# One 512-column matmul for both input parts of a feature-major weight block, the halves summed at the eviction

## The chip, the cores and the metric

One core of one Trainium2 chip runs the whole program in one launch. The metric is the device time of that launch in microseconds. TensorE (PE in the profile) multiplies, VectorE (DVE), ScalarE (ACT) and GpSimd (POOL) work on elements, and SyncE (SP) issues all DMAs.

## The reference

A block with a gated delta rule, an S5 state space part, cross attention and a SwiGLU feed-forward, then a second block with two layers (stick-breaking and block attention, then forgetting attention), each with a cross attention of four small heads and a feed-forward with a convolution. 256 positions, model width 1024, all in float32. The linear layers and feed-forwards are what the change touches:

```python
def _swiglu(hn, w_gate, w_up, w_down):
    return (jax.nn.silu(hn @ w_gate) * (hn @ w_up)) @ w_down

def conv_ffn(h, w_up, conv_w, conv_b, w_down):
    u = h @ w_up
    up = jnp.pad(u, ((0, 0), (CONV_WIDTH_2 - 1, 0), (0, 0)))
    c = conv_b
    for i in range(CONV_WIDTH_2):
        c = c + up[:, i:i + S] * conv_w[i]
    gate, val = c[..., :D_FF_2], c[..., D_FF_2:]
    return (jax.nn.silu(gate) * val) @ w_down
```

Every `hn` is a root mean square norm of the residual stream; the hidden width is 2816 = 22 tiles of 128. The other matrices are 1024 x 1024 (`w_out`, `w_xk`, `w_xq`, `w_xo`, q, k and output of the two mixers) or 1024 x 256 and 256 x 1024 (the small cross attentions), and `w_in`, `glu` and the values.

## The kernel before, in words

All activations lie feature-major in SBUF: 128 features of a tile on the partitions, T = 256 positions as columns, 8 such tiles for the model width. The weights come as 342 slots of 8 blocks of 128 x 128; SyncE loads one slot after the other in the order of use.

From `x_v` on the products keep nearly float32 accuracy by splitting. ScalarE rounds a slot to float32r (`w_hi`, L1127), VectorE subtracts that from the raw weights (`w_lo`, L1686). Every third slot's low part is made by GpSimd instead (L2500, `lo_on_pool`); in the feed-forwards that is the gate's slot. `SPLIT_SLOTS` = 3 split slots exist, so each engine's helper `ahead(s)` makes slots up to s + 2 at written places of its own order, and ScalarE waits until TensorE has read the slot three back. The inputs are split in the same way into `a_hi`, `a_lo` (tiles `AH`, `AL`) or `b_hi`, `b_lo` (`BH`, `BL`). A product of one block is three matmuls, made by `three` (L418): high weights with high input, high weights with low input, low weights with high input, all added in the same 256 columns of a PSUM bank.

A feature-major layer (`fm`, and gate and up in `ffn`) sums K input tiles (8, or 2 in `m_o0` and `m_o1`) for each of its output tiles in one bank, taken in turn from two (`acc_take` waits until the bank's last eviction). The evictions are VectorE's. In `scaled` (L1858, for q and k) and in `ffn` (L2245) one operation multiplies the bank with the norm factor `R` into SBUF; in `residual` (L2115) one adds the bank to `H`. After a residual tile ScalarE makes the next layer's `a_hi` (L1153) and the square (L1143), VectorE `a_lo` (L1698) and the sum of squares (L2105).

`ffn` goes through f = 0 to 22. TensorE's order: gate f, up f (8 blocks each), down f - 1 (8 blocks from `B`, still `three`, into banks 4 to 7). VectorE's order for f in the stages with convolution (ffn1, ffn2): evict gate; wait for ScalarE's first convolution term (L1569); two convolution steps (L2250, L2252); the same for up; product of gate and up (L2264); low part of a weight slot; low part of the activation (L2273); low part of another weight slot. ScalarE's order: first term for gate, weight copy of the next gate (which GpSimd waits for), first term for up, silu (L1574), weight copy, high part of the activation (L1584), weight copy. ffn0 has no convolution steps. Each engine runs its queue strictly in this written order; semaphores tie them. The helper `step` puts a wait on VectorE's own semaphore behind an operation, so that the next reads its result.

The functions that the diff touches:

## Time and profile before

| | us |
|---|---|
| median of 3 runs | 1260.03 |
| lowest, highest | 1256.9, 1260.96 |
| the profiled execution | 1257.22 |
| its span in the trace | 1255.3 |
| TensorE busy | 1194.8 |
| VectorE busy | 808.1 |
| ScalarE busy | 656.8 |
| GpSimd busy | 265.0 |

The stages, in us from the start of the span: w_in and the memory's small projections to 141, x_v and x_k among the delta rule to 247, w_out to 273, x_q and attention to 313, x_o to 340, ffn0 to 527, the first mixer (ab) to 640, ab_o to 665, the small cross attention to 695, ffn1 to 885, the forgetting mixer (fox) to 998, fox_o to 1020, the small cross attention to 1050, ffn2 to 1241. Busy times of matmuls overlap in the pipeline: what counts for TensorE is the distance between the starts of two matmuls.

### The profile page before, as it was taken

How to read it: one execution, taken by the hardware profiler on the slowest of the kernel's cores; microseconds unless marked ns; L12 is line 12 of the kernel's file. 1: busy time of each engine (PE TensorE's matmuls, PEld its weight loads, DVE VectorE, ACT ScalarE, POOL GpSimd, SP SyncE). 2: the span in 40 equal slices, each digit the busy share in tenths (PEclk: the TensorE clock that was granted, in tenths of full speed). 3: DMA queues.
4: the chain of work that ended last, by engine and by line, in shares of the span. 5: the costliest groups of instructions: out<-in, count | busy, mean ns of one | idle time of the engine just before them, and what ended most of it. 6: DMA issues, size and time to landing. Idle time of an engine off the chain costs nothing.

```text
span 1255.3 us, 24604 instructions
## 1 busy us (share of the span) xinstructions
PE 1194.8 (95%) x10064; PEld 1119.2 (89%) x10064; DVE 808.1 (64%) x1426; ACT 656.8 (52%) x1128; POOL 265.0 (21%) x172
## 2 busy tenths in 40 slices
PE   7999999899999999999998899999999988999997
PEld 6888778799899999998886899999889877999997
DVE  4886655564655454567866677677665576776776
ACT  3443633653644444465455655555655566555554
POOL 4030000121222322321120222322221211232231
PEclk9999899999999999999999999999999999999999
DMA  8443322353565565643343466565443342656651
GB/s 320 128 134 119 108 96 86 101 169 101 155 199 175 181 189 181 184 135 102 117 135 102 119 200 176 181 192 178 150 141 116 115 151 84 187 182 187 181 176 48
DMA packets 51518, 187.58 MB, mean 149 GB/s; under 512 B 5712, under 2 KB 5840, under 8 KB 51024
## 3 DMA queue, kind: packets, MB, share of 16 engines
q1 hardware_dynamic: 51408, 186.02, 47.8%
q8 instruction: 80, 1.31, 0.4%
q14 instruction: 30, 0.25, 0.1%
HBM read 184.95 MB, written 1.05 MB: 148 GB/s over the span
## 4 chain that ended last, share of the span: by engine, by line
PE 83%; DVE 7%; ACT 4%; issue 3%; POOL 1%; DMA 0%; DVEq 0%; SPq 0%; ACTq 0%
PE banks L418 62%; PE banks L448 7%; ACT w_hi L1127 2%; PE banks L491 2%; DVE w_lo L1686 1%; PE banks L476 1%; PE banks L924 1%; PE banks L938 1%; POOL w_lo L2500 1%; DVE h L2115 1%; PE banks L539 1%; PE banks L904 1%; DVE gates L2105 1%; PE banks L841 1%; DVE a_lo L1698 1%
## 5 line engine op out<-in xcount | busy, mean ns | idle before, releaser
L418 PE MATMUL banks<-a_hi,w_hi 128*128 128x256 f32 x1432 | 412.2, 288 | 10.1 <-ACT arena L1426 4.2
L2500 POOL TENSOR_TENSOR w_lo<-w_raw,w_hi 128x1024 fp32r<-128x1024 f32 x99 | 240.6, 2430 | 836.0 <-ACT w_hi L1127 836.0
L1127 ACT ACTIVATE w_hi<-w_raw 128x1024 fp32r<-128x1024 f32 x313 | 328.4, 1050 | 157.4 <-PE banks L418 157.3
L418 PE MATMUL banks<-a_lo,w_hi 128*128 128x256 f32 x1432 | 405.9, 283 | 0.0
L418 PE MATMUL banks<-a_hi,w_lo 128*128 128x256 f32 x1432 | 405.8, 283 | 0.0
L1686 DVE TENSOR_TENSOR w_lo<-w_raw,w_hi 128x1024 fp32r<-128x1024 f32 x214 | 264.5, 1236 | 66.7 <-ACT w_hi L1127 66.5
L418 PEld LDWEIGHTS banks<-a_hi,w_hi 128*128 128x128 f32 x1432 | 275.4, 192 | 14.9 <-ACT arena L1426 4.6
L418 PEld LDWEIGHTS banks<-a_lo,w_hi 128*128 128x128 f32 x1432 | 275.5, 192 | 0.4
L418 PEld LDWEIGHTS banks<-a_hi,w_lo 128*128 128x128 f32 x1432 | 275.3, 192 | 0.0
L418 PE MATMUL banks<-b_hi,w_hi 128*128 128x256 f32 x880 | 254.9, 290 | 16.2 <-DVE h L2115 3.9
L418 PE MATMUL banks<-b_hi,w_lo 128*128 128x256 f32 x880 | 249.9, 284 | 0.0
L418 PE MATMUL banks<-b_lo,w_hi 128*128 128x256 f32 x880 | 249.9, 284 | 0.0
L418 PEld LDWEIGHTS banks<-b_hi,w_hi 128*128 128x128 f32 x880 | 169.5, 193 | 22.4 <-issue 12.2
L418 PEld LDWEIGHTS banks<-b_lo,w_hi 128*128 128x128 f32 x880 | 169.7, 193 | 0.3
L418 PEld LDWEIGHTS banks<-b_hi,w_lo 128*128 128x128 f32 x880 | 169.6, 193 | 0.0
L1569 ACT ACTIVATE arena<-arena,pars 128x256 f32<-128x256 f32 x88 | 53.0, 602 | 132.9 <-DVE arena L2245 132.9
L2245 DVE TENSOR_TENSOR arena<-banks,rstd 128x256 f32<-128x256 f32 x132 | 55.8, 423 | 103.2 <-PE banks L418 93.4
L448 PE MATMUL banks<-early,w_raw 128*128 128x256 f32 x400 | 92.2, 390 | 7.6 <-DMA w_raw<-in_weights 7.6
L2250 DVE SCALAR_TENSOR_TENSOR arena<-arena,pars 128x255 f32<-128x255 f32 x88 | 59.1, 672 | 60.7 <-ACT arena L1569 60.7
L448 PEld LDWEIGHTS banks<-early,w_raw 128*128 128x128 f32 x400 | 77.0, 195 | 19.4 <-DMA w_raw<-in_weights 7.6
L1153 ACT ACTIVATE a_hi<-h,pars 128x256 fp32r<-128x256 f32 x64 | 32.5, 507 | 63.4 <-DVE h L2115 53.3
L1584 ACT ACTIVATE b_hi<-arena 128x256 fp32r<-128x256 f32 x66 | 27.6, 418 | 36.6 <-DVE arena L2264 36.6
(379 smaller groups left out, 1326.7 us busy)
## 6 DMA issues: line engine op xcount, KB each, us to landing
w_raw<-in_weights SPq DMA_DIRECT2D x342, 512.0 KB, 3.6
h<-in_x SPq DMA_DIRECT2D x1, 1024.0 KB, 5.1
arena<-in_mem SPq DMA_DIRECT2D x1, 1024.0 KB, 12.3
early<-in_mem SPq DMA_DIRECT2D x1, 1024.0 KB, 14.3
out_h<-h SPq DMA_DIRECT2D x4, 256.0 KB, 2.7
cons<-in_cons SPq DMA_DIRECT2D x1, 546.0 KB, 7.6
arena<-in_late SPq DMA_DIRECT2D x1, 448.0 KB, 4.2
pars<-in_pars SPq DMA_DIRECT2D x1, 290.5 KB, 2.7
```

Source lines behind the costliest of these rows:

```text
L418: ins = mm(out, l, r, start=start and n == 0, stop=stop and n == 2, skip_group_check=check)
L448: ins = mm(out, raw(s, b % 8), x[:, k, :], start=n == 0, stop=n == K - 1)
L476: ins = mm(out, x[:, k, cols], raw(s, b * w % 8, w), start=k == 0, stop=k == K - 1)
L491: ins = mm(bank[2][:, 0:T] if out is None else out, ONES_D[:] if by is None else by, squares, start=m == 0, stop=m == KD - 1)
L1127: do(WHI[:, n % SPLIT_SLOTS, :], RAW[:, n % RAW_SLOTS, :], ACT.Copy).then_inc(*inc("w_hi_made", ("w_hi", n)))
L1153: do(x[0][:, m, :], src, ACT.Copy, scale=par(g, m)).then_inc(*inc("input_hi", ("a_hi", tag, m)))
L1569: do(FC[:, 2 * (f % 2) + g, :], FS[:, 2 * (f % 3) + g, :], ACT.Identity, scale=par(f"cw{conv}", 88 + g * NF + f), bias=par(f"cb{conv}", g ...
L1584: do(BH[:, f % 3, :], FA[:, f % 2, :], ACT.Copy).then_inc(*inc("ffn_act_hi", ("act_hi", tag, f)))
L1686: v.tensor_tensor(WLO[:, n % SPLIT_SLOTS, :], RAW[:, n % RAW_SLOTS, :], WHI[:, n % SPLIT_SLOTS, :].bitcast(F32), ALU.subtract).then_inc(*i ...
L2245: v.tensor_tensor(x, acc(t)[:, 0:T], R[:], ALU.mult).then_inc(*inc("ffn_scaled", ("fs", tag, f, g), ("acc", t)))
L2250: step(v.scalar_tensor_tensor(c[:, 1:T], x[:, 0:T - 1], par(f"cw{conv}", 44 + g * NF + f), c[:, 1:T], ALU.mult, ALU.add), label="ffn_conv")
L2500: g.tensor_tensor(WLO[:, n % SPLIT_SLOTS, :], RAW[:, n % RAW_SLOTS, :], WHI[:, n % SPLIT_SLOTS, :].bitcast(F32), ALU.subtract).then_inc(*i ...
```

## The change

`AH`, `AL` become the two halves of one tile `A`, `BH`, `BL` those of `B`. A new `joint` multiplies a block's high weights with both input parts in one matmul of 2 x 256 columns, which fills a whole bank: high times high in the first half, high times low in the second. The low weights with the high input are added to the first half by a second matmul of 256 columns. All feature-major split layers use it but `glu` and `fox_f` (`ONE_HALF`); the token-major layers and the down products keep `three`. At the eviction the two halves are added: in `scaled` and `ffn` by a `tensor_reduce` over the halves from PSUM to SBUF, a wait, and then the multiplication in SBUF; in `residual` by two additions one after the other. The layers before `x_v`, with whole weights, are as before.

```diff
@@ -235,8 +235,8 @@
                 "p (a b) -> p a b", a=KD) for i in range(3))
         WHI = sb("w_hi", [P, SPLIT_SLOTS, 1024], F32R)
         WLO = sb("w_lo", [P, SPLIT_SLOTS, 1024], F32R)
-        AH, AL = sb("a_hi", [P, KD, T], F32R), sb("a_lo", [P, KD, T], F32R)
-        BH, BL = sb("b_hi", [P, KD, T], F32R), sb("b_lo", [P, KD, T], F32R)
+        A, B = (sb(n, [P, 2, KD, T], F32R) for n in ("a_parts", "b_parts"))
+        (AH, AL), (BH, BL) = ((x[:, 0, :, :], x[:, 1, :, :]) for x in (A, B))
         RAW = sb("w_raw", [P, RAW_SLOTS, 1024])
         H = sb("h", [P, KD, T])
         K1, V1 = sb("k1", [P, KD, T]), sb("v1", [P, TT, D])
@@ -292,8 +292,9 @@
 
             return bank[(6, 6, 6, 6, 6, 2, 3, 4)[p]]
 
-        A = (AH, AL)
-        B = (BH, BL)
+        def halves(key):
+
+            return acc(key).rearrange("p (a b) -> p a b", a=2)
 
 
         QKV = area(0, 12, T)
@@ -418,12 +419,19 @@
                     ins = mm(out, l, r, start=start and n == 0, stop=stop and n == 2, skip_group_check=check)
                 return ins
 
+            def joint(out, w, x, k, start, stop):
+
+
+                mm(out.rearrange("p (a b) -> p a b", a=2), w[0], x[:, :, k, :], start=start, stop=stop,
+                   skip_group_check=True)
+                return mm(out[:, 0:T], w[1], x[:, 0, k, :], start=False, stop=stop, skip_group_check=True)
+
             def blocks(s, b, n=1):
                 c = slice(b * P, (b + n) * P)
                 return WHI[:, s % SPLIT_SLOTS, c], WLO[:, s % SPLIT_SLOTS, c]
 
             def pair(x, k, cols=slice(0, T)):
-                return x[0][:, k, cols], x[1][:, k, cols]
+                return x[:, 0, k, cols], x[:, 1, k, cols]
 
             def raw(s, b, n=1):
                 return RAW[:, s % RAW_SLOTS, b * P:(b + n) * P]
@@ -432,7 +440,7 @@
 
 
                 K = SHAPE[name][0]
-                out = acc_take((name, m))[:, 0:T]
+                out = acc_take((name, m))
                 for n, k in enumerate(range(K)):
                     b = m * K + k
                     s = SLOT[name, b // 8]
@@ -445,9 +453,11 @@
                             sums(k)
                         pe.wait_ge(*at(x_ready(k)))
                     if whole(s):
-                        ins = mm(out, raw(s, b % 8), x[:, k, :], start=n == 0, stop=n == K - 1)
+                        ins = mm(out[:, 0:T], raw(s, b % 8), x[:, k, :], start=n == 0, stop=n == K - 1)
+                    elif name in ONE_HALF:
+                        ins = three(out[:, 0:T], blocks(s, b % 8), pair(x, k), n == 0, n == K - 1)
                     else:
-                        ins = three(out, blocks(s, b % 8), pair(x, k), n == 0, n == K - 1)
+                        ins = joint(out, blocks(s, b % 8), x, k, n == 0, n == K - 1)
                     ev = ([("slot", s)] if (m * K + n) % 8 == 7 else []) + ([(name, m)] if n == K - 1 else [])
                     if ev:
                         ins.then_inc(*inc("product_done", *ev))
@@ -862,12 +872,12 @@
                 for f in range(NF + 1):
                     if f < NF:
                         for g in range(2):
-                            out = acc_take((name, 2 * f + g))[:, 0:T]
+                            out = acc_take((name, 2 * f + g))
                             slot_ready(s)
                             for k in range(KD):
                                 if f == 0 and g == 0:
                                     pe.wait_ge(*at(("a_lo", tag, k)))
-                                ins = three(out, blocks(s, k), pair(A, k), k == 0, k == KD - 1)
+                                ins = joint(out, blocks(s, k), A, k, k == 0, k == KD - 1)
                             ins.then_inc(*inc("product_done", ("slot", s), (name, f, g)))
                             s += 1
                             if f == 0 and g == 0:
@@ -1146,11 +1156,11 @@
                 act.wait_ge(*at(ready))
                 if after:
                     act.wait_ge(*at(after))
-                do(x[0][:, m, :], src, ACT.Copy).then_inc(*inc("input_hi", (key, tag, m)))
+                do(x[:, 0, m, :], src, ACT.Copy).then_inc(*inc("input_hi", (key, tag, m)))
 
             def hi_gained(tag, m, x, src, g, ready):
                 act.wait_ge(*at(ready))
-                do(x[0][:, m, :], src, ACT.Copy, scale=par(g, m)).then_inc(*inc("input_hi", ("a_hi", tag, m)))
+                do(x[:, 0, m, :], src, ACT.Copy, scale=par(g, m)).then_inc(*inc("input_hi", ("a_hi", tag, m)))
 
             def rstd(tag, dst, src=None, scale=1.0, rows=slice(0, P)):
 
@@ -1695,12 +1705,12 @@
 
             def lo_gained(tag, m, x, src, g):
                 dve.wait_ge(*at(("a_hi", tag, m)))
-                v.scalar_tensor_tensor(x[1][:, m, :], src, par(g, m), x[0][:, m, :].bitcast(F32),
+                v.scalar_tensor_tensor(x[:, 1, m, :], src, par(g, m), x[:, 0, m, :].bitcast(F32),
                                        ALU.mult, ALU.subtract).then_inc(*inc("input_lo", ("a_lo", tag, m)))
 
             def lo(tag, m, x, src, key=("a_hi", "a_lo")):
                 dve.wait_ge(*at((key[0], tag, m)))
-                v.tensor_tensor(x[1][:, m, :], src, x[0][:, m, :].bitcast(F32), ALU.subtract).then_inc(
+                v.tensor_tensor(x[:, 1, m, :], src, x[:, 0, m, :].bitcast(F32), ALU.subtract).then_inc(
                     *inc("input_lo", (key[1], tag, m)))
 
             v.memset(ONES_D[:], 1.0 / D).then_inc(*inc("vector_step", "ones"))
@@ -1855,8 +1865,14 @@
             def scaled(name, m, dst, r, scale=1.0):
                 t = (name, m)
                 dve.wait_ge(*at((name, m)))
-                v.scalar_tensor_tensor(dst, acc(t)[:, 0:T], scale, r, ALU.mult, ALU.mult).then_inc(
-                    *inc("scaled_out", (name, "scaled", m), ("acc", t)))
+                if whole(SLOT[name, 0]):
+                    v.scalar_tensor_tensor(dst, acc(t)[:, 0:T], scale, r, ALU.mult, ALU.mult).then_inc(
+                        *inc("scaled_out", (name, "scaled", m), ("acc", t)))
+                    return
+                step(v.tensor_reduce(dst, halves(t).rearrange("p a b -> p b a"), AX.X, ALU.add), ("acc", t),
+                     label="halves_summed")
+                v.scalar_tensor_tensor(dst, dst, scale, r, ALU.mult, ALU.mult).then_inc(
+                    *inc("scaled_out", (name, "scaled", m)))
 
 
             turn = delta_banks(bank)
@@ -2112,7 +2128,8 @@
                     ahead(FIRST[name] + (m * K + K - 1) // 8)
                     t = (name, m)
                     dve.wait_ge(*at((name, m)))
-                    step(v.tensor_tensor(H[:, m, :], H[:, m, :], acc(t)[:, 0:T], ALU.add),
+                    step(v.tensor_tensor(H[:, m, :], H[:, m, :], halves(t)[:, 0, :], ALU.add), label="halves_summed")
+                    step(v.tensor_tensor(H[:, m, :], H[:, m, :], halves(t)[:, 1, :], ALU.add),
                          ("h", tag, m), ("acc", t), label="h_made")
                     if m:
                         lo_gained(tag, m - 1, A, H[:, m - 1, :], g)
@@ -2242,8 +2259,9 @@
                                 dve.wait_ge(*at(("fa", tag, f - 3)))
                             x = FS[:, 2 * (f % 3) + g, :]
                             t = (name, 2 * f + g)
-                            v.tensor_tensor(x, acc(t)[:, 0:T], R[:], ALU.mult).then_inc(
-                                *inc("ffn_scaled", ("fs", tag, f, g), ("acc", t)))
+                            step(v.tensor_reduce(x, halves(t).rearrange("p a b -> p b a"), AX.X, ALU.add), ("acc", t),
+                                 label="halves_summed")
+                            v.tensor_tensor(x, x, R[:], ALU.mult).then_inc(*inc("ffn_scaled", ("fs", tag, f, g)))
                             if conv is not None:
                                 c = FC[:, 2 * (f % 2) + g, :]
                                 dve.wait_ge(*at(("fc", tag, f, g)))
@@ -2579,6 +2597,8 @@
 
 SUMMED = ("xa", "f0", "xa0", "xa1")
 
+ONE_HALF = ("glu", "fox_f")
+
 POOL_SUMMED = ("mem1", "mem2")
 
 sq_before = {}
```

## Rows read from the trace of the kernel before

**Rows 1.** Page, parts 1 and 4: busy time; chain that ended last.
```profile
PE 1194.8 (95%) x10064; PEld 1119.2 (89%) x10064; DVE 808.1 (64%) x1426; ACT 656.8 (52%) x1128; POOL 265.0 (21%) x172
...
PE 83%; DVE 7%; ACT 4%; issue 3%; POOL 1%; DMA 0%; DVEq 0%; SPq 0%; ACTq 0%
```

**Rows 2.** Windows: stretch, its us, each engine's busy us, PE clock, DMA share.
```profile
340.00:527.00 187.00, 186.65 (x1546) 185.91 (x1547) 93.76 (x142) 88.01 (x119) 52.89 (x22) 1.00 0.61 185
527.00:640.00 113.00, 109.94 (x781) 96.65 (x781) 82.84 (x125) 62.91 (x110) 21.79 (x9) 1.00 0.42 124
...
695.00:885.00 190.00, 186.87 (x1551) 186.21 (x1549) 134.56 (x218) 106.50 (x156) 52.82 (x22) 1.00 0.59 175
...
1050.00:1241.00 191.00, 188.68 (x1555) 187.93 (x1553) 134.12 (x217) 106.25 (x156) 52.85 (x22) 0.99 0.53 160
```

**Rows 3.** Timeline of PE in ffn1: start, duration, operation; 256-column matmuls.
```profile
699.82 0.28 PE L418 MATMUL banks<-a_hi,w_hi 128*128 128x256 f32 x1
...
701.98 0.28 PE L418 MATMUL banks<-a_hi,w_hi 128*128 128x256 f32 x1
```

**Rows 4.** Timeline of PE in the token-major x_v: 512-column matmuls.
```profile
158.57 0.39 PE L418 MATMUL banks<-w_hi,b_lo 128*128 128x512 f32 x1
...
160.86 0.40 PE L418 MATMUL banks<-w_lo,b_hi 128*128 128x512 f32 x1
```

**Rows 5.** Timeline of VectorE, one period of ffn1.
```profile
784.17 0.42 DVE L2245 TENSOR_TENSOR arena<-banks,rstd 128x256 f32<-128x256 f32 x1 [0.16 <-PE banks L418]
785.26 0.49 DVE L2250 SCALAR_TENSOR_TENSOR arena<-arena,pars 128x255 f32<-128x255 f32 x1 [0.67 <-ACT arena L1569]
785.79 0.48 DVE L2252 SCALAR_TENSOR_TENSOR arena<-arena,pars 128x254 f32<-128x254 f32 x1
787.05 0.42 DVE L2245 TENSOR_TENSOR arena<-banks,rstd 128x256 f32<-128x256 f32 x1 [0.78 <-PE banks L418]
788.15 0.80 DVE L2250 SCALAR_TENSOR_TENSOR arena<-arena,pars 128x255 f32<-128x255 f32 x1 [0.67 <-ACT arena L1569]
...
792.81 0.42 DVE L2245 TENSOR_TENSOR arena<-banks,rstd 128x256 f32<-128x256 f32 x1 [0.17 <-PE banks L418]
```

**Rows 6.** Timeline of ScalarE in the same period.
```profile
784.63 0.60 ACT L1569 ACTIVATE arena<-arena,pars 128x256 f32<-128x256 f32 x1 [1.88 <-DVE arena L2245]
785.14 1.05 ACT L1127 ACTIVATE w_hi<-w_raw 128x1024 fp32r<-128x1024 f32 x1
```

**Rows 7.** Timeline of GpSimd in the same period.
```profile
786.26 2.40 POOL L2500 TENSOR_TENSOR w_lo<-w_raw,w_hi 128x1024 fp32r<-128x1024 f32 x1 [6.24 <-ACT w_hi L1127]
```

**Rows 8.** VectorE groups by line and shape: count, busy us, mean ns, idle.
```profile
L2264 DVE TENSOR_TENSOR arena<-arena 128x256 f32<-128x256 f32 x66 | 30.6, 464 | 6.1 <-ACT arena L1574 0.2
...
L2115 DVE TENSOR_TENSOR h<-h,banks 128x256 f32<-128x256 f32 x48 | 19.9, 415 | 7.9 <-PE banks L418 7.5
L1858 DVE SCALAR_TENSOR_TENSOR arena<-banks,rstd 128x256 f32<-128x256 f32 x44 | 18.6, 422 | 37.7 <-PE banks L418 31.9 <-ACT rstd L1160 5.6
...
L2171 DVE TENSOR_REDUCE small<-banks 128x2 f32<-128x512 f32 x12 | 8.2, 680 | 0.0
```

**Rows 9.** Line views of L2250 and L2245: minimum, median and maximum ns.
```profile
L2250 DVE SCALAR_TENSOR_TENSOR arena<-arena,pars x88: 482/486/1644, 700.0 to 1238.9; 128x255 f32<-128x255 f32 x88
...
L2245 DVE TENSOR_TENSOR arena<-banks,rstd x132: 411/424/425, 343.6 to 1237.8; 128x256 f32<-128x256 f32 x132
```

**Rows 10.** Timeline of VectorE in w_out's output and residual.
```profile
259.48 0.41 DVE L2115 TENSOR_TENSOR h<-h,banks 128x256 f32<-128x256 f32 x1
...
262.86 0.41 DVE L2115 TENSOR_TENSOR h<-h,banks 128x256 f32<-128x256 f32 x1
...
266.76 2.16 DVE L1686 TENSOR_TENSOR w_lo<-w_raw,w_hi 128x1024 fp32r<-128x1024 f32 x1 [1.18 <-ACT w_hi L1127]
268.84 0.41 DVE L2115 TENSOR_TENSOR h<-h,banks 128x256 f32<-128x256 f32 x1
```

**Rows 11.** Timeline of GpSimd in the same stretch.
```profile
265.15 2.69 POOL L2500 TENSOR_TENSOR w_lo<-w_raw,w_hi 128x1024 fp32r<-128x1024 f32 x1 [7.01 <-ACT w_hi L1127]
```

## The prediction

> **What bounds the kernel now.** I read the page first: TensorE is busy for 1194.8 of 1255.3 us and carries 83% of the chain that ended last, VectorE 7% [rows 1]. So a shorter matmul stream is worth something, if nothing else is close behind. That is a question for each stage, so next comes the windows view by stage [rows 2]: in all three feed-forward stages TensorE is busy to within 3 us of the stretch. Beside it VectorE works 93.8 of 187 us in ffn0, but 134.6 of 190 in ffn1 and 134.1 of 191 in ffn2. The third view is the timeline of one period (one hidden tile f) of ffn1 [rows 5]: the first eviction repeats after 792.81 - 784.17 = 8.64 us, exactly 72 matmuls of 0.120 us, so TensorE sets the period. What the reader should see is how little VectorE has left: its only waits for TensorE are 0.78 us before the second eviction and 0.17 us before the next first one, 0.95 us together. Its other waits (0.67 us twice) are for ScalarE's first convolution step, which itself waits for the eviction. They don't shrink when more work is put on VectorE.
>
> **What the change takes from TensorE.** Each feature-major weight block had three matmuls of 256 columns; now it has one of 512 and one of 256. A 256-column matmul starts every (701.98 - 699.82) / 18 = 0.120 us [rows 3]. A 512-column one, in the token-major layer, starts every (160.86 - 158.57) / 10 = 0.229 us [rows 4]. At 2.4 GHz (granted clock 1.00 [rows 2]) the columns alone are 0.107 and 0.213 us, so each instruction costs about 0.013 us beyond its columns, and one fewer saves 0.240 - 0.229 = 0.011 to 0.013 us. I take 0.012. Blocks: gate and up 3 x 22 x 16 = 1056; w_out, x_k, x_q, x_o, ab_o, fox_o 64 each = 384; ab_q, ab_k, fox_q, fox_k 64 each = 256; m_q0, m_o0, m_q1, m_o1 16 each = 64; in all 1760. 1760 x 0.012 = 21.1 us is all that TensorE can give back. The down products (528 blocks), glu and fox_f keep three matmuls. The new 512 columns are read from two places 2048 elements apart, which no row here shows; bounds for it are no saving at all (as if it were two matmuls) and the full one. I take the full one, because only the start of a second run changes.
>
> The Trainium skill (TensorE: Matmul & The Clock Gate, What's actually happening) gives a fixed cost of about 2.5 ns for each back-to-back matmul. By it the saving would be 1760 x 0.0025 = 4.4 us in place of 21.1. The rows show 13 ns, and I stay with them; either way it is a small term here.
>
> **What it puts on VectorE.** (a) An eviction of `ffn` or `scaled` was one operation from PSUM, 0.42 us (L1858 and L2245) [rows 8, 9]. It becomes a sum of 512 PSUM elements, then a wait on its own semaphore, then a product from SBUF. Nearest rows: a reduce of 512 PSUM elements takes 0.68 us (L2171), a 256-element product from two SBUF operands 0.43 us at its minimum (L2264, mean 0.464) [rows 8], and a step that waits for the one before starts 0.04 us after it (785.75 to 785.79) [rows 5]. So 0.68 + 0.04 + 0.43 = 1.15, or +0.73 us. The sum reads the two halves alternately; if that costs up to as much again, it is 1.2 us. From below: (0.68 - 0.42) / 256 = 1.0 ns per element between the two sizes, so 512 elements without anything fixed are 0.52. I take 0.68, since L2171 has the same count and source. The bank is free 0.26 us later than before, and the product that takes it starts over 5 us later: nothing. Behind the new wait stands the product on VectorE, and ScalarE's convolution step (L1569) waits for that; in `scaled`, the scores' matmuls. (b) A residual gets a second add, 0.415 + 0.04 = +0.45 us (L2115) [rows 8].
>
> **Where (a) lies on the path: the feed-forward with convolution.** Count from the first eviction of a period [rows 5, 6]. Before, the second convolution step ends 786.27 - 784.17 = 2.10 us after the eviction starts; after, 2.10 + 0.73 = 2.83. TensorE finishes up's product 2.8 us after gate's, so VectorE goes on without its 0.78 us wait, and the second sum runs from 2.83 to 3.51. GpSimd's share of the weight split is released by ScalarE's copy, which follows the first ScalarE convolution step (785.14 + 1.05 = 786.19); it begins at 786.26, just as the second convolution step ends [rows 5 to 7]. That order is kept, because both hang on the same ScalarE step: GpSimd reads SBUF from 2.83 to 5.23 (2.40 us). Now the new product: it has two SBUF inputs. What such an operation does beside GpSimd stands in the fifth row of [rows 5]: L2250, issued at 788.15 while GpSimd ran until 788.66 [rows 7], ended at 788.95 and took 0.80 instead of 0.49 us; its maximum is 1.64 [rows 9]. In the timeline it was long in every one of the 42 cases that met GpSimd. The old eviction, with one SBUF input, met GpSimd too (787.05) and never took more than 0.425 us in 132 [rows 9]. So the product, ready at 3.55, is held until GpSimd ends and finishes at 5.23 + 0.29 = 5.52. Then as before: 0.68 to the convolution step, 0.49 for it (it no longer meets GpSimd) = 6.69, and from its end (788.95) to where VectorE was free for the next eviction (792.64) 3.69, in all 10.38 us. TensorE needs 16 x 0.348 + 8 x 0.360 = 8.45. So VectorE sets the period: +1.7 us each, 21 periods after the first, two stages: 42 x 1.7 = +71 us. TensorE waits at the next gate's and up's low weights.
>
> The Trainium skill (SBUF — State Buffer, Who interferes with whom) states the rule behind it: a VectorE instruction with two SBUF inputs contends with a GpSimd instruction that reads SBUF, and the one that starts second is blocked entirely. It speaks against this change, and the trace agrees (0.80 and 1.64 against 0.49 us). Without that rule the sum would be the second rival below.
>
> **The other stages.** ffn0 has no convolution: VectorE's 93.8 us [rows 2] + 44 x 0.73 = 126 of 183 us, and even with a hold of 2 us in each of 22 periods 170. TensorE stays the bound: 22 x 16 x 0.012 = -4.2 us. Residuals: in w_out, three tiles take 268.84 - 259.48 = 9.36 us [rows 10] against 8.64 of TensorE, so a chain already sets the pace: residual, ScalarE's copy and square, its weight copy, the low part (on VectorE, or on GpSimd at 265.15 with the following VectorE one held to 268.92), next residual [rows 10, 11]. The add is in it twice for three tiles, and a third time where it pushes the gained low part into GpSimd's time: +0.9 to 1.3 per three tiles, +3 us for eight, four such stages: +12. m_o0 and m_o1 have products of 0.7 us a tile and VectorE nearly without pause: 8 x 0.45 less the waits, +2.5 each: +5. Where scores wait for a scaled tile at a stage's end (x_q, ab, fox, m_q0, m_q1), +0.7 each: +3. x_k and x_q save 0.8 each, given back in part: -1. In ab VectorE is busy 82.8 of 113 [rows 2]; 16 x 0.73 = 12 more, against 1.5 saved; I take +4 (between -1.5 and +12); fox has more room, 0.
> Sum: -4.2 + 71 + 12 + 5 + 3 - 1 + 4 = +90 us. The profiled execution took 1257.2 us (span 1255.3 and 1.9 around it), the median of the runs is 1260.0, so I add the sum to the first and half the difference: 1348 us.
>
> **Rivals.** (1) The sum over alternating halves is slow (1.2 us). In the convolution stages only the first of a pair lengthens the period, since the second hides beneath the hold: 42 x 0.52 = 22, and 5 elsewhere: 1375 us. Nothing in the rows speaks for it or excludes it. (2) The product isn't held. Period 2.83 + 1.15 + 0.68 + 0.49 + 3.69 = 8.84, +0.2 x 42 = 8 in place of 71: 1285 us. Against it: the 42 of 42. (3) Faster: VectorE's additions are hidden and TensorE alone counts, 1257.2 - 21.1 = 1236 us. It decides at a VectorE period under 8.45 us; even without the hold it is 8.84, so this needs operations about 0.2 us shorter each than their rows, and no GpSimd conflict. (4) The 512-column matmul runs as two: the 21.1 us aren't there, but only ffn0 and little else shows it: +6, 1354 us, inside the forecast's own range of 1320 to 1375.
>
> **How the numbers follow.** Forecast with (4) 0.72; (1) 0.12; (2) 0.11; (3) 0.05. The range 1290 to 1385 takes in the forecast, nearly all of (1) and the upper edge of (2). Under 0.3% (3.8 us), which is about what a measurement of this kernel can tell from no change, either way: 0.02, the edge between (2) and (3). Faster 0.05, slower 0.93.
>
> **What would show it.** In ffn1's timeline: starts 0.23 and 0.12 us apart on TensorE and 1 to 2 us of waiting for low weights in each period; a period near 10.4 us; the second product of a pair near 2 us long and ending 0.3 us after GpSimd, the first 0.43; ffn0 at 8.45 us a period; three residual tiles in some 10.5 us. A second product of 0.43 us makes (2) true, a reduce over 1 us (1), an unchanged period of matmul starts (4).

## The result

| | before | changed kernel |
|---|---|---|
| median | 1259.82 us (4 runs, 1256.9 to 1260.96) | 1351.56 us (4 runs, 1348.37 to 1354.01) |
| ratio of the times | | 1.0736, 95% interval 1.0709 to 1.0762 |
| span of the profiled execution | 1255.3 us | 1351.5 us |

The changed kernel is slower by 7.4%, some 92 us; the forecast was 1348 us, in a range of 1290 to 1385.

First the page of the changed kernel (parts 1 and 4: busy time by engine, and the chain that ended last), which answers to [rows 1], and the windows view of most of ffn1, to [rows 2]:

```profile
PE 1214.0 (90%) x8304; PEld 1031.7 (76%) x8304; DVE 1005.6 (74%) x1658; ACT 660.1 (49%) x1128; POOL 264.4 (20%) x172
...
PE 45%; DVE 40%; ACT 10%; issue 4%; DMA 0%; DVEq 0%; SPq 0%; ACTq 0%
```

```profile
711.00:929.00 218.00, 189.80 (x1177) 165.69 (x1176) 182.89 (x257) 102.37 (x150) 48.03 (x21) 0.99 0.46 151
```

1760 matmuls fewer, VectorE 197.5 us busier (time in which one of its operations is held counts as busy), and the chain that ended last is now VectorE's for 40% where it was 7%. In ffn1 VectorE works 182.9 of 218 us, and TensorE is no longer busy to the edge of the stretch.

One period of ffn1, VectorE's timeline (start, duration, operation), which answers to [rows 5]. L2262 is the sum of the halves, L2264 the product with the norm factor:

```profile
803.03 0.68 DVE L2262 TENSOR_REDUCE arena<-banks 128x256 f32<-128x512 f32 x1
803.75 0.42 DVE L2264 TENSOR_TENSOR arena<-arena,rstd 128x256 f32<-128x256 f32 x1
804.85 0.48 DVE L2268 SCALAR_TENSOR_TENSOR arena<-arena,pars 128x255 f32<-128x255 f32 x1 [0.67 <-ACT arena L1579]
805.37 0.48 DVE L2270 SCALAR_TENSOR_TENSOR arena<-arena,pars 128x254 f32<-128x254 f32 x1
805.77 0.68 DVE L2262 TENSOR_REDUCE arena<-banks 128x256 f32<-128x512 f32 x1
806.49 2.02 DVE L2264 TENSOR_TENSOR arena<-arena,rstd 128x256 f32<-128x256 f32 x1
809.17 0.48 DVE L2268 SCALAR_TENSOR_TENSOR arena<-arena,pars 128x255 f32<-128x255 f32 x1 [0.67 <-ACT arena L1579]
...
813.26 0.68 DVE L2262 TENSOR_REDUCE arena<-banks 128x256 f32<-128x512 f32 x1
```

GpSimd's timeline of the same period (to [rows 7]):

```profile
805.84 2.38 POOL L2518 TENSOR_TENSOR w_lo<-w_raw,w_hi 128x1024 fp32r<-128x1024 f32 x1 [7.85 <-ACT w_hi L1137]
```

TensorE's timeline, those of its rows in the period that waited:

```profile
808.37 0.47 PE L425 MATMUL banks<-a_parts,w_hi 128*128 128x512 f32 x1 [0.69 <-POOL w_lo L2518]
...
811.97 0.47 PE L425 MATMUL banks<-a_parts,w_hi 128*128 128x512 f32 x1 [0.59 <-DVE w_lo L1696]
```

The period is 813.26 - 803.03 = 10.23 us, against 8.64. No row of VectorE in it waits for TensorE any more. The second product, issued at 806.49, ends at 808.51, 0.29 us after GpSimd's operation (805.84 + 2.38 = 808.22); the first, which meets nothing, takes 0.42. TensorE is the one that waits, at the next gate's low weights from GpSimd and the next up's from VectorE.

The line views of the two operations (minimum, median, maximum ns), to [rows 9]:

```profile
L2262 DVE TENSOR_REDUCE arena<-banks x132: 676/684/693, 349.0 to 1330.8; 128x256 f32<-128x512 f32 x132
```

```profile
L2264 DVE TENSOR_TENSOR arena<-arena,rstd x132: 424/425/2520, 349.7 to 1331.6; 128x256 f32<-128x256 f32 x132
```

TensorE's timeline in ffn0, where it is the bound (to [rows 3, 4]):

```profile
449.74 0.40 PE L425 MATMUL banks<-a_parts,w_hi 128*128 128x512 f32 x1
449.98 0.28 PE L427 MATMUL banks<-a_parts,w_lo 128*128 128x256 f32 x1
450.10 0.40 PE L425 MATMUL banks<-a_parts,w_hi 128*128 128x512 f32 x1
...
450.44 0.40 PE L425 MATMUL banks<-a_parts,w_hi 128*128 128x512 f32 x1
...
450.80 0.40 PE L419 MATMUL banks<-b_parts,w_hi 128*128 128x256 f32 x2
```

A block takes (450.80 - 449.74) / 3 = 0.353 us, not the 0.348 foreseen.

And VectorE's timeline in w_out (to [rows 10]), L2131 being the first of the two adds:

```profile
260.93 0.41 DVE L2131 TENSOR_TENSOR h<-h,banks 128x256 f32<-128x256 f32 x1
261.38 0.42 DVE L2132 TENSOR_TENSOR h<-h,banks 128x256 f32<-128x256 f32 x1
```

```profile
267.72 2.59 DVE L2121 TENSOR_TENSOR gates<-gates,squares 128x256 f32<-128x256 f32 x1
...
271.37 0.41 DVE L2131 TENSOR_TENSOR h<-h,banks 128x256 f32<-128x256 f32 x1
```

Three tiles take 271.37 - 260.93 = 10.44 us there, against 9.36. L2121 is the sum of squares; beside GpSimd it takes 2.59 us.

The span by stretches, from the start of the first to the start of the last eviction of a stage (in ffn the last up's), in us. "Between" is everything else: the front, the attention parts, the small cross attentions and the ends of the feed-forwards; the lines below it are its largest differences:

| stretch | before | changed | difference | foreseen |
|---|---|---|---|---|
| ffn0 | 180.3 | 178.8 | -1.5 | -4.2 |
| ffn1 and ffn2 | 184.0, 184.2 | 217.4, 217.4 | +66.6 | +71 |
| w_out, x_o, ab_o, fox_o | 22.3, 22.5, 22.6, 20.6 | 24.5, 24.6, 24.5, 22.4 | +8.0 | +12 |
| m_o0, m_o1 | 8.9, 8.9 | 11.7, 11.3 | +5.1 | +5 |
| between | 601.1 | 619.1 | +18.0 | +6 |
| of it ahead of ab_o | 117.8 | 120.2 | +2.4 | |
| of it ahead of m_o0 | 19.8 | 21.7 | +1.9 | |
| of it ahead of fox_o | 116.3 | 121.6 | +5.3 | |
| of it ahead of m_o1 | 20.5 | 23.7 | +3.2 | |
| of it after ffn2's last eviction | 17.5 | 20.7 | +3.1 | |

### The profile page after: what moved, and what is told of

It reads as the page before. It is cut to its first block, busy times and chain, and to the rows that moved or that the text cites. A ratio compares the mean times of both kernels' runs of the same rounds, so it can differ in the third digit from the quotient of the medians.

```text
span 1351.5 us, 21316 instructions
## 1 busy us (share of the span) xinstructions
PE 1214.0 (90%) x8304; PEld 1031.7 (76%) x8304; DVE 1005.6 (74%) x1658; ACT 660.1 (49%) x1128; POOL 264.4 (20%) x172
## 4 chain that ended last, share of the span: by engine, by line
PE 45%; DVE 40%; ACT 10%; issue 4%; DMA 0%; DVEq 0%; SPq 0%; ACTq 0%
PE banks L425 11%; DVE w_lo L1696 11%; PE banks L419 11%; DVE arena L2264 8%; PE banks L456 7%; PE banks L427 5%; DVE arena L2262 4%; ACT arena L1579 4%; DVE arena L2268 3%; DVE arena L2270 3%; ACT w_hi L1137 2%; PE banks L501 1%; DVE arena L2282 1%; DVE h L2132 1%; DVE gates L2121 1%
## 5 line engine op out<-in xcount | busy, mean ns | idle before, releaser
L425 PE MATMUL banks<-a_parts,w_hi 128*128 128x512 f32 x1408 | 517.0, 407 | 59.7 <-POOL w_lo L2518 29.8
L427 PE MATMUL banks<-a_parts,w_lo 128*128 128x256 f32 x1408 | 396.2, 281 | 0.0
L425 PEld LDWEIGHTS banks<-a_parts,w_hi 128*128 128x128 f32 x1408 | 266.3, 189 | 141.1 <-issue 70.3
L427 PEld LDWEIGHTS banks<-a_parts,w_lo 128*128 128x128 f32 x1408 | 268.0, 190 | 0.5
L419 PE MATMUL banks<-b_parts,w_hi 128*128 128x256 f32 x1056 | 195.9, 286 | 14.4 <-DVE b_parts L2291 9.2
L419 PEld LDWEIGHTS banks<-b_parts,w_hi 128*128 128x128 f32 x1056 | 165.8, 193 | 18.5 <-issue 10.0
L419 PE MATMUL banks<-b_parts,w_lo 128*128 128x256 f32 x528 | 150.6, 285 | 0.0
L425 PE MATMUL banks<-b_parts,w_hi 128*128 128x512 f32 x352 | 132.8, 416 | 18.8 <-POOL w_lo L2518 9.1
L2264 DVE TENSOR_TENSOR arena<-arena,rstd 128x256 f32<-128x256 f32 x132 | 128.3, 972 | 4.6
L2262 DVE TENSOR_REDUCE arena<-banks 128x256 f32<-128x512 f32 x132 | 90.5, 686 | 47.4 <-PE banks L427 37.3
L419 PEld LDWEIGHTS banks<-b_parts,w_lo 128*128 128x128 f32 x528 | 101.8, 193 | 0.0
L427 PE MATMUL banks<-b_parts,w_lo 128*128 128x256 f32 x352 | 99.6, 283 | 0.0
L425 PEld LDWEIGHTS banks<-b_parts,w_hi 128*128 128x128 f32 x352 | 67.1, 191 | 41.3 <-issue 12.9
L427 PEld LDWEIGHTS banks<-b_parts,w_lo 128*128 128x128 f32 x352 | 67.6, 192 | 0.3
```

Source lines behind the costliest of these rows:

```text
L419: ins = mm(out, l, r, start=start and n == 0, stop=stop and n == 2, skip_group_check=check)
L425: mm(out.rearrange("p (a b) -> p a b", a=2), w[0], x[:, :, k, :], start=start, stop=stop, skip_group_check=True)
L427: return mm(out[:, 0:T], w[1], x[:, 0, k, :], start=False, stop=stop, skip_group_check=True)
L2262: step(v.tensor_reduce(x, halves(t).rearrange("p a b -> p b a"), AX.X, ALU.add), ("acc", t), label="halves_summed")
L2264: v.tensor_tensor(x, x, R[:], ALU.mult).then_inc(*inc("ffn_scaled", ("fs", tag, f, g)))
```

## The experiments

The theory: in ffn1 and ffn2 VectorE became the bound, and most of it is one operation of a period, the second product, that is held while GpSimd reads SBUF. The rivals: it is the amount of work on VectorE alone; or the 512-element sum; or TensorE. The kernel before was measured again beside each set of runs, with medians of 1255.9 to 1259.8 us, so the ratios to it say more than differences of a few us between two versions.

**The product with one SBUF input.** The same two operations of the same size, only the sum goes to a half bank of PSUM that is free in the feed-forwards:

```diff
-                            step(v.tensor_reduce(x, halves(t).rearrange("p a b -> p b a"), AX.X, ALU.add), ("acc", t),
+                            s_ = bank[3][:, g * T:(g + 1) * T]
+                            step(v.tensor_reduce(s_, halves(t).rearrange("p a b -> p b a"), AX.X, ALU.add), ("acc", t),
                                  label="halves_summed")
-                            v.tensor_tensor(x, x, R[:], ALU.mult).then_inc(*inc("ffn_scaled", ("fs", tag, f, g)))
+                            v.tensor_tensor(x, s_, R[:], ALU.mult).then_inc(*inc("ffn_scaled", ("fs", tag, f, g)))
```

> The changed kernel, but gate's and up's sum of the two halves is written to a free half bank of PSUM instead of SBUF, so that the product with the norm factor has one SBUF input; count and size of the operations are the same. Theory 1 (the product with two SBUF inputs is held by GpSimd's reading operation): every product takes 0.42 us; the hold moves on to the second convolution step of up, which still meets GpSimd's last 0.6 us, so the period of ffn1 and ffn2 falls from 10.23 to 9.1 us and the total from 1352 by 42 x 1.14 to about 1303 us. Theory 2 (it is the amount of VectorE work and the semaphore wait alone): the period stays 10.2 and the total 1352 us.

Measured: 1306.10 us, ratio to the kernel before 1.0392 (1.0375 to 1.0410) against 1.0736. Its VectorE timeline in ffn1, and GpSimd's:

```profile
784.99 0.69 DVE L2263 TENSOR_REDUCE banks<-banks 128x256 f32<-128x512 f32 x1
...
787.73 0.69 DVE L2263 TENSOR_REDUCE banks<-banks 128x256 f32<-128x512 f32 x1
788.46 0.42 DVE L2265 TENSOR_TENSOR arena<-banks,rstd 128x256 f32<-128x256 f32 x1
789.55 0.93 DVE L2269 SCALAR_TENSOR_TENSOR arena<-arena,pars 128x255 f32<-128x255 f32 x1 [0.67 <-ACT arena L1579]
...
794.10 0.69 DVE L2263 TENSOR_REDUCE banks<-banks 128x256 f32<-128x512 f32 x1
```

```profile
787.81 2.40 POOL L2519 TENSOR_TENSOR w_lo<-w_raw,w_hi 128x1024 fp32r<-128x1024 f32 x1 [6.71 <-ACT w_hi L1137]
```

The product at 788.46 runs in the middle of GpSimd's operation (787.81 to 790.21) and takes 0.42 instead of 2.02 us. The next operation with two SBUF inputs, the convolution step at 789.55, takes the hold over and ends at 790.48, 0.27 us after GpSimd. The period is 794.10 - 784.99 = 9.11 us. So 1.12 us of the 1.59 that the period grew by come from where the product's operand lies, with no work removed, and in what is left the convolution step takes 0.93 instead of 0.48 us. The rival of work alone falls.

**GpSimd's operation moved to VectorE.** In ffn1 and ffn2 the gate's low weights too are made by VectorE:

```diff
-            return (s - FIRST[name]) % 3 == 2
+            return name == "ffn0" and (s - FIRST[name]) % 3 == 2
```

> The changed kernel, but in ffn1 and ffn2 the gate's low weights are made by VectorE, not GpSimd, so nothing can hold VectorE there, and VectorE gets 1.14 us more work a period. Theory 1: the second product falls from 2.02 to 0.42 us, the period becomes 10.23 - 1.60 + 1.14 = 9.8 us, total 1352 - 42 x 0.46 = 1332 us. Theory 2 (work alone): 10.23 + 1.14 = 11.4 us a period, total 1400 us.

Measured: 1332.77 us, ratio 1.0608 (1.0590 to 1.0626). VectorE's timeline in ffn1:

```profile
786.39 0.68 DVE L2262 TENSOR_REDUCE arena<-banks 128x256 f32<-128x512 f32 x1
...
789.15 1.23 DVE L1696 TENSOR_TENSOR w_lo<-w_raw,w_hi 128x1024 fp32r<-128x1024 f32 x1
790.29 0.68 DVE L2262 TENSOR_REDUCE arena<-banks 128x256 f32<-128x512 f32 x1
791.01 0.42 DVE L2264 TENSOR_TENSOR arena<-arena,rstd 128x256 f32<-128x256 f32 x1
...
796.20 0.68 DVE L2262 TENSOR_REDUCE arena<-banks 128x256 f32<-128x512 f32 x1
```

The period is 796.20 - 786.39 = 9.81 us. VectorE got 1.2 us more to do in each period and the kernel became 19 us faster than the changed one (16 us by the ratios): the second product, with its two SBUF inputs as in the changed kernel, takes 0.42 us when GpSimd is silent.

**The two-step eviction without halves.** The kernel before, its three matmuls and its GpSimd work; only in ffn1 and ffn2 the eviction is a copy of the 256 columns and then the product:

```diff
-                            v.tensor_tensor(x, acc(t)[:, 0:T], R[:], ALU.mult).then_inc(
-                                *inc("ffn_scaled", ("fs", tag, f, g), ("acc", t)))
+                            if conv is None:
+                                v.tensor_tensor(x, acc(t)[:, 0:T], R[:], ALU.mult).then_inc(
+                                    *inc("ffn_scaled", ("fs", tag, f, g), ("acc", t)))
+                            else:
+                                step(v.tensor_reduce(x, acc(t)[:, 0:T].unsqueeze(2), AX.X, ALU.add), ("acc", t),
+                                     label="halves_summed")
+                                v.tensor_tensor(x, x, R[:], ALU.mult).then_inc(*inc("ffn_scaled", ("fs", tag, f, g)))
```

> The kernel before, three matmuls everywhere, but in ffn1 and ffn2 an eviction is two operations: a copy of the 256 columns from PSUM to SBUF (as a reduce over one element), the wait, and the product from SBUF. No halves are summed and no joint matmul exists. Theory 1 (a product with two SBUF inputs beside GpSimd): first eviction +0.47 us, second product held, period 10.23 - 0.26 = 9.97 us, total 1260 + 42 x 1.33 = 1316 us. Theory 2 (the cost is the sum over 512 elements): VectorE has 0.95 us free in a period and gets 0.94 more, the period stays 8.64 to 8.7, total 1260 to 1263 us.

Measured: 1322.32 us, ratio 1.0535 (1.0510 to 1.0559). VectorE's timeline in ffn1:

```profile
786.74 0.42 DVE L2249 TENSOR_REDUCE arena<-banks 128x256 f32<-128x256 f32 x1
...
789.20 0.42 DVE L2249 TENSOR_REDUCE arena<-banks 128x256 f32<-128x256 f32 x1
789.65 2.30 DVE L2251 TENSOR_TENSOR arena<-arena,rstd 128x256 f32<-128x256 f32 x1
...
796.72 0.42 DVE L2249 TENSOR_REDUCE arena<-banks 128x256 f32<-128x256 f32 x1
```

The period is 9.98 us: without any summing of halves 1.34 of the 1.59 us are there. The total is 66 us above the kernel before beside it (1255.90) where 56 were foreseen. The extra lies outside of the periods: ahead of fox_o 120.0 instead of 116.3 us, after ffn2's last eviction 22.0 instead of 17.5, ahead of m_o1 22.2 instead of 20.5. The last tile has no further period, so its hold and its longer chain to the down product come on top of the 21 periods, 2.0 us at each of the two ends; about as much again there, and the part ahead of m_o1, is TensorE at its lower clock, of which more below.

**What TensorE alone gives back.** The changed matmuls with the evictions of before; high weights times low input is computed, but left out at every eviction:

```diff
-                            step(v.tensor_reduce(x, halves(t).rearrange("p a b -> p b a"), AX.X, ALU.add), ("acc", t),
-                                 label="halves_summed")
-                            v.tensor_tensor(x, x, R[:], ALU.mult).then_inc(*inc("ffn_scaled", ("fs", tag, f, g)))
+                            v.tensor_tensor(x, acc(t)[:, 0:T], R[:], ALU.mult).then_inc(
+                                *inc("ffn_scaled", ("fs", tag, f, g), ("acc", t)))
...
```

(and the same in `scaled` and `residual`).

> The changed kernel with the evictions of before: only the first half of a bank is read, so high weights times low input is left out of the result, while TensorE does all of it. It shows what the matmuls alone give. Theory 1 (a 512 and a 256-column matmul take 0.353 us a block against 0.360, and where a VectorE and ScalarE chain sets the pace nothing is gained): ffn0 8.53 us a period, ffn1 and ffn2 the same, total 1260 less 66 x 0.11 and some 3 elsewhere, 1250 us. Rival (the full 0.012 us in each of 1760 blocks): 1239 us. If the joint matmul gives nothing: 1260 us.

Measured: 1246.29 us, the kernel before beside it 1256.68; ratio 0.9919 (0.9898 to 0.9940), 10 us less, as theory 1 has it, where the full saving would be 21. All three feed-forwards have a period of 8.52 us and give 2.3 to 2.5 us each; the residual stages 0.2 to 0.4 us or nothing, as is to be expected where a chain through VectorE and ScalarE sets the pace. So about 0.8% is what this change could bring here if the evictions cost nothing.

**The joint matmul as two.** The evictions as changed:

```diff
-                mm(out.rearrange("p (a b) -> p a b", a=2), w[0], x[:, :, k, :], start=start, stop=stop,
-                   skip_group_check=True)
+                mm(out[:, 0:T], w[0], x[:, 0, k, :], start=start, stop=stop, skip_group_check=True)
+                mm(out[:, T:2 * T], w[0], x[:, 1, k, :], start=False, stop=stop, skip_group_check=True)
```

> The changed kernel with the 512-column matmul done as two of 256, one into each half; all evictions as changed. Theory 1: TensorE is the bound in ffn0 alone, 8.64 instead of 8.53 us a period, +2.3 us, and up to 3 us in the q, k layers; ffn1 and ffn2 stay at 10.23; total 1355 us. Rival (the matmuls' length still counts everywhere): 1760 x 0.007 to 0.012 = +12 to +21, 1364 to 1373 us.

Measured: 1356.61 us, ratio 1.0786 (1.0761 to 1.0812). ffn0 has its 8.64 us a period again and 181.0 us in all (+2.3), ffn1 and ffn2 are unchanged at 10.23 and 217.3 us. The difference of 5 us to the changed kernel is about as wide as the two intervals, so only the stage values carry the reading: once VectorE is the bound, the saved matmuls are worth nothing.

**The change in ffn0 alone**, where VectorE has room (the evictions and the other layers follow the same choice and are left out here):

```diff
+JOINT_FFN = ("ffn0",)
...
-                                ins = joint(out, blocks(s, k), A, k, k == 0, k == KD - 1)
+                                if name in JOINT_FFN:
+                                    ins = joint(out, blocks(s, k), A, k, k == 0, k == KD - 1)
+                                else:
+                                    ins = three(out[:, 0:T], blocks(s, k), pair(A, k), k == 0, k == KD - 1)
```

> The kernel before with the joint matmul and the summed halves in ffn0 alone; all other layers have three matmuls and the old evictions. Theory 1: ffn0 is bound by TensorE, 8.53 instead of 8.64 us a period, about 1.5 us less in the stage as in the changed kernel, total 1258.5 against 1260 us, ratio 0.9988. Rival (the step from the rows before, 0.012 a block): 1255.8 us. Rival (the sums cost ffn0 too): above 1260 us.

Measured: 1256.69 us, the kernel before beside it 1255.90; ratio 1.0006 (0.9996 to 1.0016). The stage itself is 178.75 us, as in the changed kernel, against 180.28. A gain of 1.5 us (0.9988) lies outside of this interval as well as the full 4.2, so what the stage gains is not seen in the total. In the profiled executions it is lost again in a stretch whose code is the same in both kernels, ahead of m_o1. Its windows view (us, busy us of each engine, then the granted clock), first of the kernel before, then of this one:

```profile
1018.97:1039.51 20.54, 15.69 (x110) 12.14 (x108) 14.91 (x25) 12.96 (x31) 2.67 (x1) 1.00 0.30 97
```

```profile
1017.57:1040.49 22.92, 18.23 (x110) 13.66 (x108) 14.91 (x24) 13.07 (x31) 2.68 (x1) 0.85 0.27 89
```

At a mean granted clock of 0.85 instead of 1.00 the same work took 2.4 us longer. Over all runs the mean granted clock of the program was 0.990 here and 0.992 in the kernel before. Whether the change in ffn0 has a part in that stays open.

**The second add of the residuals**, left out (with it high weights times low input in those layers):

```diff
-                    step(v.tensor_tensor(H[:, m, :], H[:, m, :], halves(t)[:, 0, :], ALU.add), label="halves_summed")
-                    step(v.tensor_tensor(H[:, m, :], H[:, m, :], halves(t)[:, 1, :], ALU.add),
+                    step(v.tensor_tensor(H[:, m, :], H[:, m, :], halves(t)[:, 0, :], ALU.add),
```

> The changed kernel with one add in the residual layers: the second half of the bank is left out of the residual, so high weights times low input is missing there. By the stage times of the changed kernel the second add costs 8.0 us in w_out, x_o, ab_o and fox_o and 5.1 us in m_o0 and m_o1, and 0.4 us ahead of each next stage. Theory 1 (the add lies in the chain that sets these stages' pace): the two kinds of stage fall back to 22.3 and 8.9 us, 15 us less, 1337 us. Rival (those stages lost their time to something else, as the matmuls): no stage changes, 1352 us.

Measured: 1334.18 us, ratio 1.0604 (1.0581 to 1.0627), 17 us less than the changed kernel. w_out, x_o, ab_o, fox_o take 22.5, 22.3, 22.1, 20.3 us, m_o0 and m_o1 8.9 each: the values of before.

**q and k in one operation**, from the first half alone (the same product left out there):

```diff
-                step(v.tensor_reduce(dst, halves(t).rearrange("p a b -> p b a"), AX.X, ALU.add), ("acc", t),
-                     label="halves_summed")
-                v.scalar_tensor_tensor(dst, dst, scale, r, ALU.mult, ALU.mult).then_inc(
-                    *inc("scaled_out", (name, "scaled", m)))
+                v.scalar_tensor_tensor(dst, acc(t)[:, 0:T], scale, r, ALU.mult, ALU.mult).then_inc(
+                    *inc("scaled_out", (name, "scaled", m), ("acc", t)))
```

> The changed kernel with q and k evicted in one operation from the first half of the bank (high weights times low input is left out in x_k, x_q, ab, fox and m_q). Theory 1: in the stretches ahead of ab_o and fox_o, 2.4 and 5.2 us longer than before, about 3 us of the second is the end of ffn1 and stays, the rest goes; with x_k, x_q and m_q 5 to 7 us less in all, 1345 us. Rival (all of both stretches is the q and k evictions' doing): the stretches are as before, 10 us less, 1341 us.

Measured: 1344.16 us, ratio 1.0679 (1.0645 to 1.0712). The interval takes in both expectations, so the stretches decide: the one ahead of ab_o falls from 120.2 to 117.1 us, the one ahead of fox_o from 121.6 to 118.6, which is 2.3 us above its 116.3 of before. Not all of the last 3.0 us belongs to the evictions, as the clock below shows.

## Why the prediction was right, and where it was not

**The period of ffn1 and ffn2.** The step that carried the sum held in each of its parts: +0.72 us for the first eviction (0.68 + 0.04 + 0.42 in the rows against 0.42; +0.73 was foreseen), TensorE's wait gone, GpSimd's start just as the second sum starts, the second product held until 0.29 us after it. Foreseen 10.38 us, measured 10.23; of the 0.15, 0.09 is that the next period's sum starts before the low part ahead of it has ended (its row: 812.12, 1.23 us, so to 813.35; the sum's start 813.26), which the sum by durations left out, and 0.04 that the hold ended 5.48 instead of 5.52 us after the period's start. That makes 66.6 instead of 71 us. The Trainium skill (SBUF — State Buffer, Who interferes with whom) has the rule that a VectorE instruction with two SBUF inputs contends with a GpSimd instruction that reads SBUF, and the versions agree: with one input in PSUM 0.42 us, with GpSimd silent 0.42, otherwise 2.02 to 2.30.

**The sum over alternating halves** costs what the contiguous one did, 0.684 against 0.680 us [rows 8]: rival (1) is out. **Rival (2)**, no hold, is out by the 2.02 us. **Rival (3)** is out by the change itself; the kernel that has only its matmuls gives 1246 us, not 1236. **Rival (4)** is out by ffn0's 8.52 us.

**The matmul term was mis-sized.** I took 0.012 us a block from two streams of equal matmuls; mixed, 512 after 256 columns, a block takes 0.353 us, so it is 0.007, and ffn0 gave 1.5 us between its first and last eviction (2.3 by three matmuls against the joint one) instead of 4.2. Still, it is more than the about 0.0025 us a matmul of the Trainium skill (TensorE: Matmul & The Clock Gate, Wait — 56ns, not 53.3ns?); an estimate by it gives ffn0 a period of 8.60 us, and 8.52 was measured.

**The residuals** went nearly as described (what GpSimd holds for 2.59 us is the sum of squares, not a low part), with 10.44 us for three tiles (foreseen 10.3 to 10.7), but over the eight tiles of four stages +8.0 instead of +12: the stages grew by 0.9 us for three tiles on average (2.0 in seven intervals), the lower end of the range, and I had multiplied by eight tiles where seven intervals count. m_o0 and m_o1 +5.1 against +5. That the add lies on the chain is shown by the kernel without it.

**The rest, +18 instead of +6**, is the step that failed, and in three ways.

First, I counted the periods of the convolution stages but not what follows the last of them. From the last sum to the down product that needs it takes 5.98 us instead of 3.98 after ffn2 and 6.55 instead of 4.55 after ffn1: the hold and the longer chain once more, 2.0 us at each end.

Second, the prediction has no term for TensorE's clock. The end of ffn2, before and after: the row of the first down matmul with the wait ahead of it, and the window from there to the start of the norm's sums (the last number but two is the mean granted clock):

```profile
1241.74 0.36 PE L418 MATMUL banks<-b_hi,w_hi 128*128 128x256 f32 x1 [1.14 <-DVE b_lo L2273]
```

```profile
1241.74:1244.70 2.96, 2.96 (x25) 2.96 (x26) 1.83 (x5) 2.10 (x5) 0.00 (x0) 1.00 0.00 0
```

```profile
1336.82 0.47 PE L419 MATMUL banks<-b_parts,w_hi 128*128 128x256 f32 x2 [4.07 <-DVE b_parts L2291]
```

```profile
1336.82:1341.16 4.34, 4.34 (x25) 4.34 (x26) 2.52 (x6) 2.85 (x7) 0.00 (x0) 0.63 0.01 4
```

The same matmuls take 1.4 us longer, because most of them run at a granted clock of 0.5 (1.2 GHz). TensorE had waited for 4.07 us just before, against 1.14. The end of ffn1 is alike: a wait of 4.64 against 1.71 us, then 5.85 against 4.34 us. The lower clock shows in this place after both stages in all seven kernels that lengthen this wait, and in none of the three that don't (the kernel before, the one with one-step evictions, the one with only ffn0 changed); that the wait is the cause was not tested by itself. So the end of ffn2 costs 3.1 us by 2.0 of chain and 1.4 of clock, less 0.2 behind them.

The forgetting mixer lost 1.8 us to the clock as well. The window from the end of ffn1's down products to fox_o, in the changed kernel and in the one with the sum in PSUM, whose code there is the same:

```profile
940.99:1050.15 109.16, 105.50 (x668) 85.50 (x667) 77.04 (x125) 57.28 (x124) 19.90 (x8) 0.98 0.37 121
```

```profile
918.46:1025.80 107.34, 103.90 (x668) 84.55 (x667) 76.84 (x126) 57.22 (x124) 19.91 (x8) 1.00 0.38 123
```

The kernel before took 107.41 us there. So q's and k's two-step evictions cost nothing net in fox, as foreseen, and +2.4 in ab (120.2 against 117.8, at clock 1.00 in both), where I had +4. Ahead of m_o1 the kernel before had clock 1.00 and the changed one, like the one with only ffn0 changed, a lower one: 2.4 of the 3.2 us are there without the change. What brought the clock down in these two places isn't shown.

Third, +1.9 ahead of m_o0 and some 2 us of small differences elsewhere stay unexplained.

The misses and the two overestimates nearly cancel in the total (+92 by the medians, +96 by the profiled spans, +90 foreseen). The mechanism and its 67 of the 96 us were right; that the total came within a few us is luck.

No version that computes everything beats the kernel before. With the evictions free the gain would be 10 us, and the one stage with room, ffn0, shows nothing in the total that can be measured.

## What to carry to other kernels

Before an operation is split in two, ask where the second half's operands lie: reading PSUM it ran through GpSimd's work in 0.42 us, reading two SBUF tiles it stood for 2 us, once in each period of the busiest stages. Count the follower's slack in the loop (0.95 us of 8.64 here), not its busy share (71%): 1.46 us more and the bound has changed engines, and every further saving on the old one is worth nothing. Where a stage is a loop of periods, count its end too, and ask what TensorE's clock does after a longer wait: at the end of ffn2 2.0 us more of chain came with 1.4 us of slower matmuls.

## What the runs showed that was not expected

Giving VectorE 1.2 us more work a period made the kernel 19 us faster, because the work was taken from the engine that held it up. And the saving of the joint matmul shrank when matmuls of two lengths alternate: 0.353 us for a pair, where two streams of one length each gave 0.229 + 0.120 = 0.349 [rows 3, 4].
